# Sharing a stationary operand between two products: (k, q) with k in the delta rule, (values, ones) with keys in the matrix memory, and other shares of the filler

## The reference, cut to what matters

```
# matrix memory (mlstm_scan)
P   = einsum('bhtd,bhsd->bhts', qc, kc) * exp(D - mt)
num = einsum('bhts,bhsv->bhtv', P, vc) + w_st * einsum('bhtk,bhkv->bhtv', qc, C)
den = sum(P, -1) + w_st * einsum('bhtk,bhk->bht', qc, n)
h   = num / maximum(abs(den), exp(-mt))
C   = wc * C + einsum('bhs,bhsk,bhsv->bhkv', ws, kc, vc)
n   = wc * n + einsum('bhs,bhsk->bhk', ws, kc)
# gated delta rule (gdn_scan)
kk  = einsum('bhtd,bhsd->bhts', kc, kc)
A   = eye + where(strict, beta * kk * decay, 0)      # solved against (v, k)
qk  = einsum('bhtd,bhsd->bhts', qc, kc) * decay
```

## Time and profile before

| | us |
|---|---|
| median of three runs | 2336.99 |
| lowest and highest of them | 2336.76, 2339.62 |
| profiled execution, its own time | 2338.52 |
| its span, first to last instruction | 2336.4 |
| PE busy | 2227.1 (95%) |
| DVE, ACT, POOL busy | 903.7, 803.7, 668.1 |
| mean granted clock of TensorE | 0.971 |

### The profile page before, as it was taken

One profiled execution on the slowest core, in us unless ns is written; L12 is line 12 of the kernel. 1 busy time (PEld: TensorE's weight loads), 2 busy tenths in 40 slices (PEclk: granted clock), 3 DMA queues, 4 the chain that ended last, 5 costly groups with the idle time before them and its releaser, 6 DMA issues.

```text
span 2336.4 us, 36746 instructions
## 1 busy us (share of the span) xinstructions
PE 2227.1 (95%) x14018; PEld 2159.0 (92%) x14018; DVE 903.7 (39%) x1357; ACT 803.7 (34%) x1442; POOL 668.1 (29%) x469
## 2 busy tenths in 40 slices
PE   7999999999998999999999799979999999999997
PEld 6999999999798999899998798979999999999997
DVE  5886233332655563144433356243221211212215
ACT  5555222322455453133331233224223133132232
POOL 1449422222444442211222122211212212212121
PEclk9999999998899999799998899989999999999999
DMA  4233646432233323245441644310111101101112
GB/s 170 57 92 94 185 138 181 125 102 82 83 107 110 104 73 119 82 134 168 143 127 48 203 168 137 109 48 23 59 36 45 58 31 49 58 27 54 53 33 88
DMA packets 191534, 222.03 MB, mean 95 GB/s; under 512 B 38670, under 2 KB 146226, under 8 KB 191334
## 3 DMA queue, kind: packets, MB, share of 16 engines
q1 hardware_dynamic: 168476, 181.91, 25.9%
q10 hardware_dynamic: 22986, 39.13, 4.7%
HBM read 162.22 MB, written 58.77 MB: 95 GB/s over the span
## 4 chain that ended last, share of the span: by engine, by line
PE 78%; DVE 10%; POOL 3%; issue 3%; DMA 2%; ACT 2%; SPq 1%; DVEq 0%; ACTq 0%; POOLq 0%
PE D L373 66%; DVE g_dq L915 1%; DVE m_rd L1971 1%; POOL b_t L678 1%; POOL b_u L675 1%; PE M L814 1%; POOL w_lo L354 1%; DVE u_x L487 1%; PE M L1752 1%; DVE g_lg L1103 1%; DVE xn_lo L2270 1%; DMA proj<-stage 0%; DVE acc L2265 0%; PE M L1841 0%; ACT g_sg L846 0%
## 5 line engine op out<-in xcount | busy, mean ns | idle before, releaser
L373 PE MATMUL D<-xn_hi,w_hi 128*128 128x352 f32 x2760 | 925.2, 335 | 40.9 <-ACT stage L392 16.5
L373 PE MATMUL D<-xn_hi,w_lo 128*128 128x352 f32 x2760 | 897.7, 325 | 0.0
L373 PE MATMUL D<-xn_lo,w_hi 128*128 128x352 f32 x2760 | 896.4, 325 | 0.0
L373 PEld LDWEIGHTS D<-xn_hi,w_hi 128*128 128x128 f32 x2760 | 526.8, 191 | 64.2 <-issue 24.1
L373 PEld LDWEIGHTS D<-xn_lo,w_hi 128*128 128x128 f32 x2760 | 529.0, 192 | 4.7 <-issue 3.8
L373 PEld LDWEIGHTS D<-xn_hi,w_lo 128*128 128x128 f32 x2760 | 526.5, 191 | 0.0
L354 POOL TENSOR_TENSOR w_lo<-w_raw,w_hi 128x1024 fp32r<-128x1024 f32 (+1 forms) x105 | 248.1, 2363 | 679.8 <-ACT w_hi L348 679.8
L354 POOL TENSOR_TENSOR w_lo<-e,w_hi 128x512 fp32r<-128x512 f32 (+1 forms) x96 | 164.1, 1710 | 607.7 <-ACT w_hi L348 607.7
L373 PE MATMUL D<-y_hi,w_hi 128*128 128x352 f32 x960 | 311.9, 325 | 17.9 <-DVE y_lo L2339 14.4
L373 PE MATMUL D<-y_lo,w_hi 128*128 128x352 f32 x960 | 311.9, 325 | 0.0
L373 PE MATMUL D<-y_hi,w_lo 128*128 128x352 f32 x960 | 311.3, 324 | 0.0
(11 more groups left out here) (458 smaller groups left out, 2424.5 us busy)
## 6 DMA issues: line engine op xcount, KB each, us to landing
w_raw<-in_w_proj SPq DMA_DIRECT2D x73, 512.0 KB, 3.8
proj<-stage ACTq DMA_DIRECT2D x60, 528.0 KB, 3.2
e<-in_w_full SPq DMA_DIRECT2D x32, 512.0 KB, 3.5
e<-in_w_half SPq DMA_DIRECT2D x64, 256.0 KB, 2.6
stage<-proj SPq DMA_DIRECT2D x24, 528.0 KB, 3.6
d_bc<-rowd SPq DMA_DIRECT2D x32, 256.0 KB, 5.8
m_in<-proj SPq DMA_DIRECT2D x32, 256.0 KB, 3.8
proj<-u_o SPq DMA_DIRECT2D x12, 528.0 KB, 2.9
```

The source lines that it names most:

```text
L373: last = nc.tensor.matmul(D[b][:, 0:GN], w[t.slot][:, k, :], x[:, k, cols], start=(k == 0 and n == 0), stop=(k == kt - 1 and n == 2))
```

## The change

1. In the delta rule, k against k and q against k become one product per head of 256 columns: (q, k) move past the stationary k. The results of two heads share a bank, in a new allocation `MM` that spans the banks M2 to M4; DVE reads them through a view (`by_k`). The prompt and the sample both use it.
2. In the matrix memory's prompt loop, the transposed values are kept at a pitch of 129 with a column of ones behind each head's 128 (written once by a memset). `kv` has 129 columns per head, over the banks M3 and M4, two heads in each, and `kn` is gone. DVE adds C and n from there. `ss` goes to M0 instead of M4. The sample keeps the old layout and its own `kn`.
3. `ML_SLOTS` goes from six equal shares to `[3, 3, 4, 3, 3, 2]`; ACT empties the bank of the group before (`slot.evacuate()`) ahead of its wait for h.

```
-        M = [... psum_tensor(f"M{i}", [P, 512], F32) for i in range(6)]
+        M01 = [... psum_tensor(f"M{i}", [P, 512], F32) for i in range(2)]
+        MM = ctx.enter_context(nc.psum_tensor("MM", [P, 3 * 512], F32))
+        M = M01 + [MM[:, i * 512:(i + 1) * 512] for i in range(3)] + [... "M5" ...]
...
+            def by_k(x):
+                return MM[0:N, 0:2 * C4].rearrange("p (h x n) -> p h x n", x=2, n=N)[:, :, x, :]
...
-                eng.tensor_tensor(sq(B.lt), sq(M[2]), sq(B.db), ALU.mult).then_inc(*dve_.step("lt"))
+                eng.tensor_tensor(sq(B.lt), by_k(1), sq(B.db), ALU.mult).then_inc(*dve_.step("lt"))
...
-                eng.tensor_tensor(sq(B.at), sq(M[3]), sq(B.de), ALU.mult).then_inc(*dve_.step("qkd"))
+                eng.tensor_tensor(sq(B.at), by_k(0), sq(B.de), ALU.mult).then_inc(*dve_.step("qkd"))
...
                 for h in range(H):
-                    for q in range(2):
-
-                        i = eng.matmul(M[2 + q][0:N, h * N:(h + 1) * N], hn(B.qk, C4)[:, h, :], hn(B.qk, (1 - q) * C4)[:, h, :], start=True, stop=True)
+                    q_and_k = B.qk[:, 0:2 * C4].rearrange("p (x h n) -> p x h n", x=2, n=N)[:, :, h, :]
+                    i = eng.matmul(MM[0:N, h * 2 * N:(h + 1) * 2 * N].rearrange("p (x n) -> p x n", n=N), hn(B.qk, C4)[:, h, :], q_and_k, start=True, stop=True)
...
+            def vt_of(h):
+                return tk(m_vt, h) if sample else m_vt[:, h * (HD + 1):h * (HD + 1) + HD]
+
+            def with_n(lo, hi):
+                two = MM[:, 512:3 * 512].rearrange("p (a f) -> p a f", f=512)[:, :, 0:2 * (HD + 1)]
+                return two.rearrange("p a (b c) -> p a b c", c=HD + 1)[:, :, :, lo:hi]
...
-                    eng.wait_ge(*pe_.after("kn", n))
-                    eng.tensor_tensor(m_C[:, :], m_C[:, :], M[3][:, :], ALU.add).then_inc(*dve_.step("c2"))
-                    eng.tensor_tensor(m_N[:, :], m_N[:, :], M[0][:, 0:H], ALU.add).then_inc(*dve_.step("n2"))
+                    eng.wait_ge(*pe_.after("kv", n))
+                    c4 = m_C[:, :].rearrange("p (a b v) -> p a b v", b=2, v=HD)
+                    eng.tensor_tensor(c4, c4, with_n(0, HD), ALU.add).then_inc(*dve_.step("c2"))
+                    n4 = m_N[:, :].rearrange("p (a b) -> p a b", b=2)
+                    eng.tensor_tensor(n4, n4, with_n(HD, HD + 1).squeeze(3), ALU.add).then_inc(*dve_.step("n2"))
...
-                eng.activation(m_vt[0:N, :], M[5][0:N, :], ACT.Copy).then_inc(*act_.step("vt"))
+                if sample:
+                    eng.activation(m_vt[0:N, 0:N4], M[5][0:N, :], ACT.Copy).then_inc(*act_.step("vt"))
+                else:
+                    eng.activation(m_vt[:, 0:H * (HD + 1)].rearrange("p (h c) -> p h c", c=HD + 1)[:, :, 0:HD],
+                                   M[5][:, :].rearrange("p (h c) -> p h c", c=HD), ACT.Copy).then_inc(*act_.step("vt"))
                 slot()
                 if sample:
                     for _ in range(3):
                         slot()
+                else:
+                    slot.evacuate()
...
                     for h in range(H):
-                        i = eng.matmul(M[3][:, h * HD:(h + 1) * HD], tk(m_kt, h), tk(m_vt, h), start=True, stop=True)
+                        i = eng.matmul(with_n(0, HD + 1)[:, h // 2, h % 2, :], tk(m_kt, h), m_vt[:, h * (HD + 1):(h + 1) * (HD + 1)], start=True, stop=True)
                     i.then_inc(*pe_.step("kv"))
-                    for h in range(H):
-                        i = eng.matmul(M[0][:, h:h + 1], tk(m_kt, h), ones[:, 0:1], start=True, stop=True)
-                    i.then_inc(*pe_.step("kn"))
                 slot()
                 eng.wait_ge(*act_.after("sq", n))
-                i = eng.matmul(M[4][:, 0:C4], ones, m_sq[:, 0:C4], start=True, stop=True)
+                i = eng.matmul(M[0][:, 0:C4] if not sample else M[4][:, 0:C4], ones, m_sq[:, 0:C4], start=True, stop=True)
...
-        ROW_SLOTS, ML_SLOTS = [9, 2, 4, 3], 6
+        ROW_SLOTS, ML_SLOTS = [9, 2, 4, 3], [3, 3, 4, 3, 3, 2]
...
+            eng.memset(m_vt[:, 0:H * (HD + 1)].rearrange("p (h c) -> p h c", c=HD + 1)[:, :, HD:HD + 1], 1.0).then_inc(ready, 1)
```

More of the change, by code:

```diff
@@ L284, in build @@
             m_ks, m_e, m_pt, m_so, m_gw, m_qw, m_vt, m_kt, m_dn, m_rd, m_h, m_sq, m_y, m_C, m_qn = [
-                arena(a, f"m_{n}", [P, N4]) for n in ("ks", "e", "pt", "so", "gw", "qw", "vt", "kt", "dn", "rd", "h", "sq", "y", "C", "qn")]
+                arena(a, f"m_{n}", [P, N4 + 8 * (n == "vt")]) for n in ("ks", "e", "pt", "so", "gw", "qw", "vt", "kt", "dn", "rd", "h", "sq", "y", "C", "qn")]
             m_in = arena(a, "m_in", [P, 4 * N4])
@@ L288, in build @@
             mx_bc = arena(a, "mx_bc", [P, 3 * H * NS])
-            arena(a, "m_gap", [P, 13568 - 10624])
+            arena(a, "m_gap", [P, 13568 - 10632])
             m_bc = arena(a, "m_bc", [P, 3 * N4])
@@ L307, in build @@
         D = [ctx.enter_context(nc.psum_tensor(f"D{i}", [P, 512], F32)) for i in range(2)]
-        M = [ctx.enter_context(nc.psum_tensor(f"M{i}", [P, 512], F32)) for i in range(6)]
+        M01 = [ctx.enter_context(nc.psum_tensor(f"M{i}", [P, 512], F32)) for i in range(2)]
+        MM = ctx.enter_context(nc.psum_tensor("MM", [P, 3 * 512], F32))
+        M = M01 + [MM[:, i * 512:(i + 1) * 512] for i in range(3)] + [ctx.enter_context(nc.psum_tensor("M5", [P, 512], F32))]
         const_ld, masks_ld = sem("const_ld"), sem("masks_ld")
@@ L1000, in tk @@
             def tk(x, h=None):
-                v = x[0:N, :].rearrange("p (h n) -> p h n", n=HD)
+                v = x[0:N, 0:N4].rearrange("p (h n) -> p h n", n=HD)
                 return v if h is None else v[:, h, :]
@@ L1868, in build @@
         mx_in, mx_st = sem("mx_in"), sem("mx_st")
-        ml_pe = steps("ml_pe", "vt kq kt num den kv kn ss", credit=1)
+        ml_pe = steps("ml_pe", "vt kq kt num den kv ss", credit=1)
         ml_act = steps("ml_act", "ks e0 e1 e2 e3 s1 s2 s3 vt sq rl rr", credit=1)
@@ L2047, in mlstm @@
                 eng.wait_ge(*pe_.after("ss", n))
-                eng.activation(m_sq[:, 0:C4], M[4][:, 0:C4], ACT.Ln, bias=EPS, scale=1.0 / HD).then_inc(*act_.step("rl"))
+                eng.activation(m_sq[:, 0:C4], M[4][:, 0:C4] if sample else M[0][:, 0:C4], ACT.Ln, bias=EPS, scale=1.0 / HD).then_inc(*act_.step("rl"))
                 eng.wait_ge(*act_.after("rl", n))
@@ L2079, in mlstm @@
                 for h in range(H):
-                    i = eng.matmul(M[1][:, h * N:(h + 1) * N], tk(m_vt, h), sq(m_pt, h), start=(not sample or h == 0), stop=False, skip_group_check=sample)
+                    i = eng.matmul(M[1][:, h * N:(h + 1) * N], vt_of(h), sq(m_pt, h), start=(not sample or h == 0), stop=False, skip_group_check=sample)
                     if sample:
```

## The result

| five executions of each | median us | lowest to highest |
|---|---|---|
| before | 2336.76 | 2333.39 to 2339.62 |
| after | 2320.09 | 2314.91 to 2325.94 |

The ratio is 0.9929, with a 95% interval of 0.9913 to 0.9946: the changed kernel was 16.7 us faster in this series. The forecast was 8.5 us faster, 2328.5 us, with a range from 2324 to 2334; the measured time lies outside it. Three more series of the same two kernels gave ratios of 0.9947 [0.9930, 0.9965], 0.9962 [0.9939, 0.9985] and 0.9948 [0.9929, 0.9967].

The account below looks back on a forecast made before the run. The prediction took TensorE, 78% of the chain, to bound the kernel, except where a DVE/ACT chain covers its work. Terms of 7.7, 0.6 and 0.2 summed to 8.5 us, from 2336.99 to 2328.5 us, range 2324 to 2334.

Parts of the forecast that it names:

- The bound and the two parts of a chunk: Matrix-memory loop: `den` to `ss`, 7.15 us, is set by DVE and ACT; `ss` to `den`, 23.95 us, by PE.
- kn at price 0: Matrix-memory loop: removing kn's 0.89 us of PE a chunk only lengthens the wait ahead of `ss`, gaining 0.
- The moved piece, 7.7 us: Matrix-memory loop: six more filler matmuls between kv and `ss` save 0.97 us a chunk, 7.7 us in eight.
- What the piece needs: Matrix-memory loop: banks are emptied in time, 0.9 us to spare at the tightest; DVE opens chunks 1.4 us before PE.
- Rival A: Matrix-memory loop: the stop moves to a bank or the chunk's start, eating up to the whole 0.97; 2336.2 us, chance 0.10.
- The delta rule, 0.6 and 0.2: Delta rule: merging kk and qk saves 0.6 us in the prompt's eight chunks and 0.2 us in the sample.
- B: Matrix-memory loop: kn's 0.89 and the wait's 0.96 vanish together, 15.6 us in all, 2321.4 us; chance 0.04.
- C: Matrix-memory loop: the odd pitch slows L2080's 64 weight loads by 0.111 us each, 7.1 us back, 2335.6 us; chance 0.05.
- D: TensorE's clock behind the loop: shifted low-clock dips move time some 3 us, up to 8 (2320.5 to 2336.5); larger swings 0.09.

Follow-up runs that it names:

- five pieces: Changed kernel with filler shares [3, 3, 5, 2, 3, 2] and ACT emptying group 2's bank ahead of `ss`; 2320.74 and 2315.97 us, ratios 0.9938 and 0.9914.

## Why the prediction was wrong, point by point

**The bound and the two parts of a chunk: right.** `den` to `ss` stayed at 7.14 us in the changed kernel. From record to record it is 7.31 in the kernel before, in the changed one and without the shares, whatever PE did beside it, and longer only where PE's own work outlasts the chain: 7.49 with the shares alone, 7.96 with five pieces.

**kn at price 0: right to 1 us.** Without the shares its 0.89 went into the wait (0.96 to 1.86), and with them it brought the wait back from nothing to 0.90. The loop is 0.1 to 0.8 us shorter with it than with the shares alone, not 7.1.

**The moved piece, 7.7 us: right in mechanism, mis-sized by a little.** With all edits the loop is 7.8 to 8.9 us shorter, depending on the profile (248.4 and 248.9 against 240.0 to 240.6); the shares alone give 7.7 at equal clock. The chunk lost 1.11 instead of 0.97 because the 66 matmuls behind `ss` ran at 0.159 each and not at 0.161; the kernel before shows both paces in its own chunks (11.45 and 11.60 for 72), so this is no effect of the change.

**What the piece needs: right, but by less than the text thought.** No bank, load or y stalled PE. The cover at the chunk's start was read from one opening, 2.67 before, and put at 1.4 after; in that opening it came out above that, but the thinnest of the loop, 1.46 before, fell to 0.75 and in another profile to 0.19. There SP issues the sample's loads (mx_h, mx_bc) while yd is under way, before and after; that they delay yd isn't shown. Rival A was nearer than the 1.4 us said.

**The delta rule, 0.6 and 0.2: right for the first** (0.07 a chunk, and 0.8 ± 0.6 for the edit alone), **0.05 instead of 0.2 for the sample.**

**Rivals.** A didn't come. B gave nearly the measured time, 2321.4, and was wrong all the same: the shares alone, with kn still there, bring the chunk to 30.08, and without the shares kn's time shows in the wait. A total near a rival's is no evidence for its mechanism while the clock can move it by as much. C is out: the weight loads from a pitch of 129 kept their pace, 0.22 for two. Each takes 0.192 us before and after. The prediction's estimate of 3% from the lines of the Trainium skill ("SBUF — State Buffer", "Door 1: The DMA port swizzle") doesn't show in them. That page's warning of PSUM patterns that aren't contiguous isn't tested: each matmul of kv writes its 129 columns side by side.

**The step that failed is D's size,** "The three runs of before span 2.9 us. It shifts the result by some 3 us either way, up to 8", and with it the range; the larger swings had a chance of 0.09, and 2320.09 lies just beyond their 2320.5. The 82 executions of the same kernel span 21 us, the 29 of the changed one 25. Three executions were no measure of that. The profile of before, at a clock of 0.971, was itself a low draw: its stretch from 541 to 995, clock 0.93, is the longest of that stretch that any run shows. D also looked in the wrong place: it let the stages behind the loop swing because they begin 8.5 us sooner. Behind the loop the two first profiles differ by 0.8 us; 12.2 lie ahead of it, where nothing had moved, and the same stretch differs as much between two executions of one program. The sum of the work, 8.5, stands at 8.4 ± 0.4 at equal clock; the other 8 us of the first series are 6.7 by its clock and a kernel before that lay 1 us high. That they aren't work of the edits follows from two things that were seen: the matrix memory's loop, at the full clock, repeats to 0.6 us over the profiles of one program while the stretch with low clock differs by 12.3 us between two executions of one program, in step with its time at half clock; and time follows the mean granted clock at one slope in all kernels.

**What stays open.** Over 29 and 82 executions the changed kernel keeps a mean granted clock 0.002 higher, about 4 us, more than its standard error of 0.0005. The shares alone don't show it (0.9732 ± 0.0006), and the kernels with some of the merged products lie between (0.9735 each, ± 0.0007; five pieces 0.9738 ± 0.0005, though that kernel holds all the edits). No run names the edit. As for the stretch, the changed kernel's four profiles have 27 to 34 us at half clock between the delta rule's sample and the matrix memory, and the kernel before's two have 41 and 61, while both take 1090 to 1093 us behind the loop; but one profile of the shares alone has 20, so these few don't prove it. The Trainium skill ("TensorE: Matmul & The Clock Gate", "What's actually happening") has the gate follow the array's recent activity; the low stretches of this trace agree with that. In the first profile of the kernel before those between 541 and 1600 lie in or behind the three samples, with their products of 4 and 32 columns, and otherwise beside stops of PE: at 749 and 800 in HGRN2's prompt loop (stops of 5.5 and 2.0 us), at 1360, 1412 and 1558 (2.0, 3.4 and 3.1 us). Why they are fewer in one kernel these runs don't show.

## What to carry to other kernels

Cut a loop's period into the part that another engine's chain sets and the part that the busiest engine sets: work removed beside the chain only lengthens a wait, and filler moved out of the other part into that wait is worth its full time, until the wait is gone. Read a cover in every chunk of the loop: the thinnest one was half of the one that the prediction read. Where the matrix engine's clock dips in quiet stretches, the time of one program is a distribution; learn its width before giving a range, and compare kernels at equal mean granted clock or by the stretches that run at the full clock. A total that agrees with a theory proves it only once the stretches agree too.

## What the runs showed of the hardware

One program spread over 21 us (82 executions) and another over 25 (29), 1%, with the mean granted clock between 0.969 and 0.981, 2.1 us for each 0.001. A weight load from rows of 516 bytes and a matmul with 129 fp32 columns into PSUM at an odd column showed no price (0.11 us each, as with 128; the load 0.192 before and after).
